# First quarter of the adaptive modulation multiplied on TensorE in column groups of 32, and the squares of x issued ahead of the copy of the eigenvalues

## What is computed

```python
cond = jax.nn.silu(c)                        # 1024 numbers
mod = cond @ w_ada[l] + b_ada[l]             # 1024 x 3072
shift, scale, gate = jnp.split(mod, 3, axis=-1)
h = rms_norm(x, norm_g[l]) * (1.0 + scale[:, None, :]) + shift[:, None, :]
proj = h @ w_in[l]
...
lam = lax.complex(a_re.astype(jnp.float32), a_im.astype(jnp.float32))   # s5_mixer: 32 groups of 64 eigenvalues
dt = jnp.exp(log_dt.astype(jnp.float32))[:, None]
lam_bar = jnp.exp(lam * dt)
```

## Time and profile before

| what | value |
|---|---|
| time, median of 3 runs | 1311.62 us (1311.55 to 1311.70) |
| the profiled execution: its own time, its span | 1311.51 us, 1309.7 us |
| PE busy | 1277.3 us (98%), granted clock 1.00 |
| DVE busy | 945.7 us (72%) |
| ACT busy | 373.0 us (28%) |
| DMA over the span | 120.67 MB, 92 GB/s |

### The profile page before, as it was taken

One profiled execution on the slowest core, in us unless ns is written; L12 is line 12 of the kernel. 1 busy time (PEld: TensorE's weight loads), 2 busy tenths in 40 slices (PEclk: granted clock), 3 DMA queues, 4 the chain that ended last, 5 costly groups with the idle time before them and its releaser, 6 DMA issues.

```text
span 1309.7 us, 17546 instructions
## 1 busy us (share of the span) xinstructions
PE 1277.3 (98%) x6256; PEld 919.6 (70%) x6256; DVE 945.7 (72%) x2163; ACT 373.0 (28%) x926; POOL 277.2 (21%) x264
## 2 busy tenths in 40 slices
PE   4999999999999999999999999999999999999998
PEld 3444455544788876875455556888888888888887
DVE  5898999679786897564556677675867767786563
ACT  4223121225311112232556675110232232220000
POOL 1168578215103668700000000001000000000000
PEclk9999999999999999999999999999999999999999
DMA  9773524660412132112112003113223223233210
GB/s 317 201 152 111 154 42 134 186 209 10 161 39 79 65 112 82 65 33 97 65 23 44 1 2 65 65 65 112 66 75 119 65 94 100 65 113 129 89 48 33
DMA packets 91041, 120.67 MB, mean 92 GB/s; under 512 B 16488, under 2 KB 52654, under 8 KB 90956
## 3 DMA queue, kind: packets, MB, share of 16 engines
q1 hardware_dynamic: 86256, 110.81, 27.5%
q10 hardware_dynamic: 2956, 5.05, 1.2%
q0 software_dynamic: 1744, 3.70, 1.0%
HBM read 111.00 MB, written 6.84 MB: 90 GB/s over the span
## 4 chain that ended last, share of the span: by engine, by line
PE 89%; DVE 7%; issue 1%; ACT 1%; DMA 1%; ACTq 0%; DVEq 0%; POOL 0%; POOLq 0%
PE bank L1582 18%; PE bank L1608 10%; PE bank L1243 9%; PE bank L933 8%; PE bank L920 8%; PE bank L1510 7%; PE bank L1468 6%; PE bank L955 5%; PE bank L1348 4%; PE bank L1420 3%; PE bank L1448 3%; PE bank L1553 2%; PE bank L984 1%; PE bank L1090 1%; DVE arena L2752 1%
## 5 line engine op out<-in xcount | busy, mean ns | idle before, releaser
L1582 PE MATMUL bank<-arena 128*128 128x256 f32 x1120 | 241.9, 379 | 0.0
L1582 PEld LDWEIGHTS bank<-arena 128*128 128x128 f32 x1120 | 212.8, 190 | 28.9
L1608 PE MATMUL bank<-arena 128*128 128x256 f32 x616 | 133.1, 379 | 0.0
L1608 PEld LDWEIGHTS bank<-arena 128*128 128x128 f32 x616 | 117.0, 190 | 15.9
L955 PEld LDWEIGHTS bank<-arena 128*128 128x128 f32 (+2 forms) x660 | 77.6, 143 | 71.8 <-issue 44.1
L933 PE MATMUL bank<-arena 128*128 128x512 f32 x288 | 127.7, 596 | 0.0
L1243 PE MATMUL bank<-arena 128*128 128x256 f32 x560 | 122.4, 380 | 0.0
L1243 PEld LDWEIGHTS bank<-arena 128*128 128x128 f32 x560 | 106.0, 190 | 15.1 <-issue 0.7
L955 PE MATMUL bank<-arena 128*128 128x128 f32 (+2 forms) x660 | 92.7, 278 | 21.8 <-ACT arena L1692 7.4
L3154 DVE CUSTOM_DVE_ANT_0 arena<-bank,arena 128x128 f32<-128x128 f32 (+3 forms) x128 | 57.5, 487 | 66.1 <-PE bank L1420 64.8
L920 PE MATMUL bank<-arena 128*128 128x512 f32 (+1 forms) x256 | 102.2, 552 | 0.0
(11 more groups left out here) (398 smaller groups left out, 2010.9 us busy)
## 6 DMA issues: line engine op xcount, KB each, us to landing
arena<-in_w_in SPq DMA_DIRECT2D x14, 2048.0 KB, 7.8
arena<-in_w_up SPq DMA_DIRECT2D x20, 1024.0 KB, 6.9
arena<-in_w_ada SPq DMA_DIRECT2D x16, 512.0 KB, 9.1
arena<-in_w_down SPq DMA_DIRECT2D x8, 1024.0 KB, 8.0
arena<-in_w_out SPq DMA_DIRECT2D x2, 2048.0 KB, 10.5
arena<-in_w_attn_br SPq DMA_DIRECT2D x8, 512.0 KB, 7.9
arena<-in_w_o SPq DMA_DIRECT2D x2, 2048.0 KB, 8.6
rb_dram<-rb_one_dram ACTq DMA_DIRECT2D x1, 2560.0 KB
```

The source lines that it names most:

```text
L1582: mm = pe.matmul(ps, left[:, k, :], right[:, k, :], start=(first and k == 0), stop=(k == 3), skip_group_check=True)
L1608: mm = pe.matmul(down_acc(i, name), left, right, start=first and name in ("P1", "P7", "P2", "P4"), stop=last, skip_group_check=True)
```

## The change

Four edits.

1. A tile `silw` of 128 x 8 x 32: DVE zeroes it and writes silu(c) to its column 0 for each k; so each `silw[:, k, :]` is a weight matrix of 32 columns of which one isn't zero.
2. `mod_rows()` on PE, between the turns `("x", 3)` and `("x", 4)`: eight matmuls 128x32 by 128x512 with `adaS[0]` as the moving operand, for k = 0 to 7 into the PSUM partitions 32 (k mod 4) onwards of bank 2, the second four added to the first. DVE then copies the bank to `macc[0]` instead of the eight operations of `mod_sums(0)`. `mod_turn(0)` is as before.
3. ACT squares x first and copies the eigenvalues after that; DVE waits for that copy behind its exponential instead of ahead of it.
4. `"msum"` takes a running number, so that all later users of the banks 4 to 7 move by one bank.

```diff
+        silw = arena[:, BASE + 6144:BASE + 6400].rearrange("p (k n) -> p k n", k=KT)
...
-        name_aux(*[("x", k) for k in range(KT)])
+        name_aux(*[("x", k) for k in range(4)])
+        name_aux("msum", banks=2)
+        name_aux(*[("x", k) for k in range(4, KT)])
...
                 for k in range(KT):
+                    if k == 4:
+                        mod_rows()
                     turn((key, k), [src[:, t, 128 * k:128 * k + 128] for t in range(TT)])
+
+            def mod_rows():
+
+                ps = begin_aux("msum")
+                pe.wait_ge(silc_done, 1)
+                for k in range(KT):
+                    if k % 4 == 0:
+                        pe.wait_ge(ada_in[0][k // 4], 32)
+                    c = 32 * (k % 4)
+                    mm = pe.matmul(ps[c:c + 32, :], silw[:, k, :], adaS[0][:, k, :], start=(k < 4), stop=(k >= 4),
+                                   skip_group_check=True)
+                mm.then_inc(aux_done, 1)
...
-            aux_ready(act, "lam")
-            act.activation(sp[:, 2:4, :], abank("lam")[:, 0:64].rearrange("p (a b) -> p a b", a=2), ACT.Copy)\
-               .then_inc(afree("lam"), 1)
             for t in range(TT):
                 act.wait_ge(x_in[t], 16)
                 if t:
                     act.wait_ge(sq_done, t)
                 act.activation(sqx, xrow[:, t, :], ACT.Square, accum_out=stat[:, t:t + 1]).then_inc(sq_done, 1)
+            aux_ready(act, "lam")
+            act.activation(sp[:, 2:4, :], abank("lam")[:, 0:64].rearrange("p (a b) -> p a b", a=2), ACT.Copy)\
+               .then_inc(afree("lam"), 1)
...
-            v.tensor_scalar(silc[:, 0:8], silc[:, 0:8], 0.5, None, ALU.mult).then_inc(silc_done, 1)
+            step(v.memset(silw, 0.0))
+            v.tensor_scalar(silw[:, :, 0], silc[:, 0:8], 0.5, None, ALU.mult)
+            step(v.tensor_scalar(silc[:, 0:8], silc[:, 0:8], 0.5, None, ALU.mult))
+            v.sem_inc(silc_done, 1)
...
-            aux_out(v, "lam")
             v.wait_ge(ldt_in, 16)
             exp_(t_(DT), t_(LDT))
+            aux_out(v, "lam")
             mul(t_(XR), t_(LR), t_(DT))
             mul(t_(TH), t_(LI), t_(DT))
-            mod_sums(0)
+            aux_ready(v, "msum")
+            v.tensor_copy(macc[0], abank("msum")[:, :]).then_inc(macc_done, 1)
+            v.wait_ge(macc_done, 1)
+            v.sem_inc(afree("msum"), 1)
```

## The result

The changed kernel is slower: 1316.67 us median of 10 runs (1314.69 to 1318.86) against 1313.60 for 10 runs of before (1311.29 to 1315.52). The two medians lie 3.1 us apart and the means 3.6; the ratio is 1.003, 95% interval 1.0021 to 1.0039, that is +3.9 us, +2.8 to +5.1. The profiled execution took 1315.22 us with a span of 1313.4, that is +3.7 us in the span.

The account below looks back on a forecast made before the run. PE was taken to bound the kernel (89% of the chain), with the removed DVE work hidden. Matmuls 2.05 + eigenvalue copy 0.15 - squares 0 - DVE 0 = +2.2 us, giving 1313.8; range 1312.0 to 1316.0.

Parts of the forecast that it names:

- The removed DVE work is worth nothing: DVE at the start: 6.06 us of removed work was hidden under ACT's scalings and PE's transposes, so gain 0.
- The squares gain 0: ACT at the start: landings of x's third and fourth tiles pace the squares; gain 0 to 0.1 us, taken as 0.
- (D): Rival: earlier landings of x, or matmuls filling PE's waits, cancel the cost; -0.5 to +1.5 us, 1311.1 to 1313.1; chance 0.10.
- The copy of the eigenvalues, 0.15: ACT, between fourth square and first scaling: the copy now stands on the chain and costs 0.1 to 0.25, taken as 0.15 us.
- The eight matmuls, 2.05: `mod_rows` on PE: two sets of four side by side, 1.95 us, plus 0.1 for array-mode changes; bounds 1.8 and 3.
- DVE's copy 0.7, small steps in time, no wait of SP, moved banks free: Around `mod_rows`: copy and small steps covered by turns 4 to 7, SP margin 1.1 us, moved banks free; no cost.
- Sum at `mod_turn(0)`: PE at the start: matmuls 2.05 plus eigenvalue copy 0.15 give +2.2 us; `mod_turn(0)` near 25.0 instead of 22.84.
- "What the start loses or gains should arrive at the end one for one.": First 25 us to the end: nearly no transfer behind the start could swallow a shift, so +2.2 us arrives whole.
- "1311.5 becomes 1313.7; the median of the runs lies 0.1 above it.": Whole kernel: the profiled execution's own time plus 2.2 us, then 0.1 for the median of the runs, giving 1313.8.
- Rival (B): PE at the start: `mod_rows` falls into the slow pace of the first transposes, +2 us more, 1315.8; chance 0.13.

Follow-up runs that it names:

- dense: Kernel before plus two unused 512-column matmuls over the full array between turns 3 and 4 of x: 1317.34 against 1311.99, ratio 1.0036.
- filled pause: Kernel before plus two unused matmuls in PE's 1.3 us pause behind `mod_turn(0)` and the bucket rows: 1312.47 against 1313.35, ratio 0.9999.
- matmuls alone: Changed kernel with the squares back behind the copy of the eigenvalues: 1316.56 against 1311.99 of before, ratio 1.0035.
- tiny: Kernel before plus eight unused one-column PE matmuls, ahead of x's turns (1315.27 against 1313.56, ratio 1.0012) or the h group's first product (one run, 1313.12).
- one group: Changed kernel with all eight `mod_rows` matmuls chained into the same 32 PSUM partitions: 1321.34 against 1311.99 of before, ratio 1.0067.
- delayed kernel: Kernel before plus two unused 768-column squares on ACT ahead of the squares of x, PE's program untouched: 1315.29 against 1312.52, ratio 1.0021.
- the pause filled: Changed kernel plus two unused matmuls in PE's 1.3 us pause ahead of the first product with u's weights: 1317.14 against 1313.35 of before, ratio 1.003.
- half of the rows early: Changed kernel with the `mod_rows` matmuls of k = 0 to 3 moved ahead of the turns of x: 1316.52 against 1313.35 of before, ratio 1.0025.

## Why the prediction was wrong

Step by step:

- **The removed DVE work is worth nothing.** Right: DVE idled 8.57 us where `mod_sums(0)` had been, and two dense matmuls with `mod_sums(0)` kept gave the same time.
- **The squares gain 0.** Right: ratio 0.9999 with them alone. The first transpose came 0.3 us early, but that isn't the edit's: in the profiles in which ACT's part is that of before, it lies at 16.86 (dense), 17.11 (filled pause), 17.24 (matmuls alone), 17.59 and 17.74 (tiny), against 17.63. So the landings vary between executions, and the start of the transposes with them by 0.9 us: in the dense kernel the third tile of x lands at 10.23, where before had it at 11.0, and not the eigenvalues but this tile is what the squares wait for. Under (D) the prediction took the close agreement of three runs as a sign against this.
- **The copy of the eigenvalues, 0.15.** 0.11 in the chain.
- **The eight matmuls, 2.05.** 1.85 measured; 7.08 in one group. The 0.1 that I added for the change between the full array and groups isn't there.
- **DVE's copy 0.7, small steps in time, no wait of SP, moved banks free.** Right: 0.69; SP's issues of `w_ada` went on without a gap from 12.06 to 30.31.
- **Sum at `mod_turn(0)`.** 2.2 forecast, 1.77 measured: right mechanism, 0.4 too much, of which 0.3 is the earlier first transpose.
- **"What the start loses or gains should arrive at the end one for one."** This step failed. It holds for a pure shift (2.1 us on ACT arrived as 2.1 in the profile) but not for added PE work. Two things came on top in the profile, +0.85 net from 3.4 us at half clock behind the pause and +1.1 from the late landing at 519 us: 1.77 + 0.85 + 1.1 = 3.7. In six of ten runs the clock was lower still, 0.996 or 0.997.
- **"1311.5 becomes 1313.7; the median of the runs lies 0.1 above it."** This failed too, as a term that the prediction took from too little: three runs within 0.15 us. Ten runs of before have a median of 1313.60, 2.0 us higher, and on the four chips of the experiments it is 1312.0 to 1313.6. Of the 2.9 us between 1313.8 and 1316.67, 2.0 is this level and 0.9 the difference of the medians over the forecast (3.1 instead of 2.2). Neither alone would have left the range: the level of ten runs with +2.2 gives 1315.8, the old level with +3.1 gives 1314.7, or 1315.5 with the +3.9 of the ratio.
- **Rival (B)** had the slow pace of PE as what would add 2 us, with 0.13, but inside `mod_rows`. `mod_rows` ran at full pace; the loss came 4 us later, in work that the change doesn't touch. The measured time lay just above the range, whose upper end was built on (B) alone, without the drop, the landing or a higher level of before.

The Trainium skill ("TensorE: Matmul & The Clock Gate", Part 1) says that PE idle for long enough goes back to 1.2 GHz. The traces here need something beside that: the same pause of 1.3 us kept the clock at 1.00 in before and in the delayed kernel and was followed by 0.50 in the changed one, and with the pause filled the clock fell at 61 us in the midst of work.

**Open.** What decides where the clock falls. It fell behind the pause when the pause began 8.1 to 8.4 us after the first transpose (dense, matmuls alone, changed) and at 7.7 (tiny matmuls), and didn't at 6.3 (before), 6.5 (delayed) or 13.8 (one group); but at 7.0 it stayed with the squares alone and fell with half of the rows early, and the places at 57 to 68, 291 and 535 us aren't covered. One profile per kernel shows one execution, and the clocks of the other runs differ from it. What makes the load at 517 us late is open too. No kernel tried here beats before by more than the noise.

## What to carry to other kernels

Moving hidden work from an engine that has slack to the one on the critical path costs its full duration, however well it is packed there; look first whether the operations removed stand in the chain at all. Column groups are a good tool where the matmuls must run (3.8 times as fast here), and the place for them is idle time of PE, as the first half ahead of the turns showed (1.2 us saved at `mod_turn(0)`). For effects of a few microseconds, compare the mean granted clock of the runs beside their times: runs of before alone went from 1310.8 us at 1.000 to 1316.7 at 0.996, and one profile doesn't show that. For the same reason a forecast of a time needs more than three runs behind its starting level; here three lay within 0.15 us and 2.0 us under the median of ten.

## What the hardware showed that I had not expected

- TensorE's clock fell to half for 3 to 10 us in a PE stream that was busy 98% of the span: from 27, 57, 61, 291 or 535 us on in the profiles of kernels that differ by a few matmuls at the start, and nowhere while PE worked in before's. Runs with a mean clock of 0.997 to 0.995, which most kernels had, lose up to 0.3 to 0.5% of their time to it.
- The first transposes after 7 us of idle time take 0.204 us each and the later ones 0.118, while the granted clock reads 1.00 all along; the quicker pace came after 3 us (before) or some 6 us (eight tiny matmuls added). The column doesn't show all of it.
- Two or more matmuls added to PE's program anywhere ahead of it made a load of 2048 KB at 517 us land 1.1 to 1.7 us later (7.6 to 7.8 against 8.75 to 9.34 us), with 0.8 to 1.1 us of that on the path.
